# A third place for output panels, doubled weight chunks, and refills at the head of their step in a two-layer encoder trunk

## What is computed

```python
def sq_relu_mlp(h, w_up, w_down):            # d_ff = 4096
    u = relu(h @ w_up)
    return (u * u) @ w_down

# layer 0
x = x + diff_attention(rms_norm(x, attn_norm_g[0]), a_w_qkv, ...)   # 8 heads, ends in  o @ a_w_o
x = x + sq_relu_mlp(rms_norm(x, mlp_norm_g[0]), mlp_w_up[0], mlp_w_down[0])
# shared keys and values
k, v = split(rms_norm(x, kv_norm_g) @ w_kv);  k = rms_norm(k, kv_k_norm_g)
# layer 1
x = x + swa_sink_attention(rms_norm(x, attn_norm_g[1]), b_w_q, ..., b_w_o, k, v)  # 4 groups of 4 query heads
x = x + sq_relu_mlp(rms_norm(x, mlp_norm_g[1]), mlp_w_up[1], mlp_w_down[1])
```

## Time and profile before

| | us |
|---|---|
| median of 3 runs | 2355.66 (2349.65 to 2358.06) |
| the profiled execution | 2355.31 |
| its span, first to last instruction | 2353.6 |
| mean granted clock of PE | 0.975 of full |

### The profile page before, as it was taken

One profiled execution on the slowest core, in us unless ns is written; L12 is line 12 of the kernel. 1 busy time (PEld: TensorE's weight loads), 2 busy tenths in 40 slices (PEclk: granted clock), 3 DMA queues, 4 the chain that ended last, 5 costly groups with the idle time before them and its releaser, 6 DMA issues.

```text
span 2353.6 us, 36507 instructions
## 1 busy us (share of the span) xinstructions
PE 2222.9 (94%) x11916; PEld 1909.4 (81%) x11916; DVE 1593.7 (68%) x3173; ACT 1162.1 (49%) x2483; POOL 842.2 (36%) x1464
## 2 busy tenths in 40 slices
PE   6999999976999999899999989998999999899998
PEld 5999999965878888788777988887878888778777
DVE  5688888763576666776776368875576666776773
ACT  4566666653455455533444256653455555543342
POOL 2333333343642222332334155554542233232331
PEclk9999999977999999999999899997999999999999
DMA  6111000002424444762452110003424444663352
GB/s 197 35 28 28 27 27 21 1 19 93 130 82 148 149 153 161 258 241 84 149 197 90 36 37 10 10 19 99 129 87 155 162 158 162 249 223 104 135 173 82
DMA packets 186756, 255.86 MB, mean 109 GB/s; under 512 B 15072, under 2 KB 135904, under 8 KB 181984
## 3 DMA queue, kind: packets, MB, share of 16 engines
q1 hardware_dynamic: 186592, 253.82, 32.3%
HBM read 174.09 MB, written 79.69 MB: 108 GB/s over the span
## 4 chain that ended last, share of the span: by engine, by line
PE 80%; DVE 10%; issue 5%; ACT 3%; DMA 1%; POOLq 1%; POOL 0%; DVEq 0%; SPq 0%; ACTq 0%
PE score L1855 45%; PE trb L1855 13%; PE proj L1855 13%; PE pv L1855 5%; DVE xop L1350 3%; DVE w_op L1350 1%; PE trb L2205 1%; PE trb L1893 1%; ACT p L960 1%; DVE xT L1591 1%; DVE p L1488 1%; DMA w_quad<-in_mlp_w_down 1%; DVE pb L1802 1%; ACT pb L1315 1%; PE trb L1945 0%
## 5 line engine op out<-in xcount | busy, mean ns | idle before, releaser
L1855 PE MATMUL score<-xop,w_op 128*128 128x512 f32 x3840 | 893.8, 392 | 25.3 <-DVE xop L1350 12.6
L1855 PEld LDWEIGHTS score<-xop,w_op 128*128 128x128 f32 x3840 | 720.8, 189 | 185.3 <-issue 36.1
L799 POOL TENSOR_TENSOR w_quad<-w_quad,w_sum 128x512 f32<-128x512 f32 x64 | 99.5, 1555 | 807.1 <-DVE w_op L1350 807.1
L1855 PE MATMUL trb<-xop,w_op 128*128 128x512 f32 x1536 | 361.9, 390 | 5.4 <-DVE w_op L1350 2.0
L1855 PEld LDWEIGHTS trb<-xop,w_op 128*128 128x128 f32 x1536 | 287.4, 188 | 68.8 <-issue 5.8
L923 ACT ACTIVATE w_op<-w_quad 128x512 fp32r<-128x512 f32 (+1 forms) x336 | 216.3, 645 | 247.0 <-PE score L1855 165.3
L1350 DVE TENSOR_TENSOR w_op<-w_quad,w_op 128x512 fp32r<-128x512 f32 (+1 forms) x336 | 285.0, 852 | 43.8 <-ACT w_op L923 43.8
L1591 DVE TENSOR_TENSOR xT<-score,xT 128x512 f32<-128x512 f32 x160 | 109.8, 686 | 159.0 <-PE score L1855 150.9
L1855 PE MATMUL score<-a_hi,w_op 128*128 128x512 f32 x512 | 162.1, 397 | 3.8 <-DVE w_op L1350 3.8
L960 ACT ACTIVATE p<-p,nm_a,slopes 128x128 f32<-128x128 f32 (+7 forms) x124 | 106.6, 861 | 112.6 <-DVE nm_a L1493 110.4
L1350 DVE TENSOR_TENSOR xop<-xop 128x1024 fp32r<-128x1024 f32 x112 | 143.3, 1290 | 16.3 <-ACT xop L923 16.3
(11 more groups left out here) (266 smaller groups left out, 4567.1 us busy)
## 6 DMA issues: line engine op xcount, KB each, us to landing
xop<-u_dram SPq DMA_DIRECT2D x112, 512.0 KB, 5.8
u_dram<-quad SPq DMA_DIRECT2D x32, 1536.0 KB, 9.7
w_quad<-in_mlp_w_up SPq DMA_DIRECT2D x64, 512.0 KB, 5.3
w_quad<-in_mlp_w_down SPq DMA_DIRECT2D x64, 512.0 KB, 4.9
wa_raw<-in_a_w_qkv SPq DMA_DIRECT2D x96, 128.0 KB, 2.4
quad<-xT_dram SPq DMA_DIRECT2D x32, 256.0 KB, 4.2
xT_dram<-xs SPq DMA_DIRECT2D x32, 256.0 KB, 2.6
u_dram<-quad SPq DMA_DIRECT2D x32, 256.0 KB, 4.0
```

The costliest lines, as they stand in the source:

```text
L799: return pool.tensor_tensor(out, x, y, ALU.subtract)
L1855: return nc.tensor.matmul(out, a, b, start=start, stop=stop, **kw)
```

## The change

In four parts.

**Panels.** The split weights have three places, in slots (2, 3), (0, 1) and (5, 6) of `w_op`, and the results three pairs of banks, the third made of `proj` and `pv`. PE may begin panel i once panel i - 3 has been added. Panel 2 of layer 0 is split at the end of the first attention. The split of a panel moves one panel earlier in ACT's and DVE's order, and its load with it. The last panel is done by halves: first the 24 matmuls of tokens 512 to 1023, then those of the first half, of which 16 read only `a_hi` and the last 8 read `a_lo`. The weights of the MLP's products 3 and 4 (ACT) and 3 (DVE) and the scaling of the last panel's second half move ahead of its first half, and slots 2 and 3 of `xop23` are released at the end of the `a_hi` products.

**Weight chunks.** Chunks 0 to 5 of odd jobs live in `wo_b`, so chunks 0 to 5 of a job are split while the job before runs (in one piece for jobs 1 and 2, two chunks in each of steps 2, 3 and 4 for jobs 3 to 5), and chunks 6 and 7 where all eight stood.

**Refills.** Each half slot from the fourth on stands a step earlier, apart from those that share one, and in its step the refill stands first on ACT, and on DVE behind the additions and ahead of `op_of_weights`.

**Loops.** The `Fori` over groups 1 and 2 is written out.

```diff
@@ refill_at
-    steps = (1, 2, 4, 5, 6, 7, 8, 8, 9, 10, 11, 11, 12, 13)
+    steps = (1, 2, 4, 4, 5, 6, 7, 7, 8, 9, 10, 10, 11, 12)
@@ tiles and banks
-        w_hi = [w_op[:, 2 * i, :, :].rearrange("p a (k n) -> p (a k) n", n=P) for i in range(2)]
-        w_lo = [w_op[:, 2 * i + 1, :, :].rearrange("p a (k n) -> p (a k) n", n=P) for i in range(2)]
+        w_hi = [w_op[:, i, :, :].rearrange("p a (k n) -> p (a k) n", n=P) for i in (2, 0, 5)]
+        w_lo = [w_op[:, i, :, :].rearrange("p a (k n) -> p (a k) n", n=P) for i in (3, 1, 6)]
+        wo_bank = [bank[0], bank[1], [proj[:, :], pv[:, :]]]
+        def halves_of(i):
+            return (1, 0) if i == KC - 1 else (0, 1)
+        def wb_rows(part, k, job):
+            if job % 2 and k < 6:
+                return wo_b[:, k // 2, part, 256 * (k % 2):256 * (k % 2 + 1)]
+            return (wb_hi, wb_lo)[part][:, k, :]
@@ sync, segment
                 load_wo(0)
                 load_wo(1)
+                load_wo(2)
                 if seg == 0:
-                    load_wo(2)
                     load_wo(3)
...
+                if seg:
+                    load_wo(3)
                 for i in range(KC):
-                    if i + 2 < KC and (seg or i >= 2):
-                        load_wo(i + 2)
+                    if 1 <= i < KC - 3:
+                        load_wo(i + 3)
@@ scalar
             square_outputs(NH * 4, 1, NB - 2)
+            split_panel(2)
             evac_o(last_uses, NH - 1)
-            def wb_split(job, gain):
+            def wb_split(job, gain, first=0, end=KC):
                 act.wait_ge(wb_in, job * 16 + 16)
-                if not isinstance(job, int) or job > 0:
-                    act.wait_ge(pb_ready, job * NB)
-                for k in range(KC):
-                    copy(wb_hi[:, k, :], wb_raw[:, k, :], gains[:, gain, k:k + 1]).then_inc(wb_hi_done, 1)
+                if first < 6 and job == 1:
+                    act.wait_ge(prod, OPS)
+                elif first < 6 and job > 1:
+                    act.wait_ge(pb_ready, (job - 1) * NB)
+                for k in range(first, end):
+                    if k == 6 and job > 0:
+                        act.wait_ge(pb_ready, job * NB)
+                    copy(wb_rows(0, k, job), wb_raw[:, k, :], gains[:, gain, k:k + 1]).then_inc(wb_hi_done, 1)
@@ scalar, segment (vector alike)
-                for i in range(KC):
-                    if i + 1 < KC and (seg or i):
-                        panel = KC * seg + i + 1
-                        split_panel(panel, panel // 2, panel % 2)
-                    if i == KC - 1:
-                        for k in range(3):
-                            op_of_weights(k)
-                        for slot in range(2):
-                            for u in (2, 3):
-                                unit_hi(u, slot)
+                if seg:
+                    split_panel(KC * seg + 1)
+                for i in range(KC - 1):
+                    if i + 2 < KC and (seg or i):
+                        split_panel(KC * seg + i + 2)
                     scaled(i)
-                    if i < KC - 1:
-                        squares(i)
+                    squares(i)
...
-                unit_hi(2, 2)
-                op_of_weights(3)
-                unit_hi(3, 2)
-                op_of_weights(4)
-                squares(KC - 1)
+                for k in range(5):
+                    op_of_weights(k)
+                scaled(KC - 1, (1,))
+                for slot in range(3):
+                    for u in (2, 3):
+                        unit_hi(u, slot)
+                scaled(KC - 1, (0,))
...
                 for k in range(OPS + 6):
+                    for s, h in refill_at(k):
+                        refill_hi(s, h)
                     n = (k + 1) // 7 if k else 0
...
                     if k + LEAD + 1 < OPS:
                         op_of_weights(k + LEAD + 1)
-                    for s, h in refill_at(k):
-                        refill_hi(s, h)
@@ scalar, after segment 0, and steps (vector alike)
+                if s == 5:
+                    wb_split(1, 3, 0, 6)
+            wb_split(1, 3, 6)
...
-                        if s == NB - 2 and more:
-                            wb_split(g + 3, 4)
+                        if s in (2, 3, 4, NB - 2) and more:
+                            wb_split(g + 3, 4, *((6, KC) if s == NB - 2 else (2 * s - 4, 2 * s - 2)))
...
-            with act.Fori(1, KVH - 1) as g:
+            for g in range(1, KVH - 1):
@@ vector, MLP step
+                    for s, h in refill_at(k):
+                        refill_lo(s, h)
                     if k < 4:
                         for u in (2, 3):
                             unit_lo(u, 3 + k)
                     if k + LEAD < OPS:
                         op_of_weights(k + LEAD)
...
-                    for s, h in refill_at(k):
-                        refill_lo(s, h)
@@ tensor
+            def last_panel(slot):
+                out, w_h, w_l = wo_bank[slot], w_hi[slot], w_lo[slot]
+                for k in range(KC):
+                    last = three(out[1], (w_h[:, k, :], w_l[:, k, :]), (a_hi[:, k, HALF:S], a_lo[:, k, HALF:S]),
+                                 k == 0, k == KC - 1)
+                last.then_inc(panel_half, 1)
+                for k in range(KC):
+                    mm(out[0], w_h[:, k, :], a_hi[:, k, 0:HALF], k == 0, False)
+                    last = mm(out[0], w_l[:, k, :], a_hi[:, k, 0:HALF], False, False)
+                    if k in (3, KC - 1):
+                        last.then_inc(wo_half, 1)
+                for k in range(KC):
+                    last = mm(out[0], w_h[:, k, :], a_lo[:, k, 0:HALF], False, k == KC - 1)
+                last.then_inc(panel_half, 1)
...
-                    if i >= 2:
-                        pe.wait_ge(xs_ready, 16 * seg + 2 * i - 2)
+                    if i >= 3:
+                        pe.wait_ge(xs_ready, 16 * seg + 2 * i - 4)
```

More of the change, by code:

```diff
@@ L601, in segment @@
                         load_unit(u)
-                    for half in range(2):
-                        sp.wait_ge(xs_ready, 16 * seg + 2 * i + half + 1)
+                    for j, half in enumerate(halves_of(i)):
+                        sp.wait_ge(xs_ready, 16 * seg + 2 * i + j + 1)
                         sp.dma_start(x_dram[:, i, HALF * half:HALF * (half + 1)], xs[:, half, :])\
@@ L1137, in squares @@
                 def squares(i):
-                    for half in range(2):
+                    if i == KC - 1:
+                        act.wait_ge(panel_half, 2 * KC * (seg + 1))
+                    for half in halves_of(i):
                         if i % 2 and i < KC - 1:
@@ L1581, in _, with wb_split @@
             o_factors(NH, 1)
-            def wb_split(job, gain):
-                for k in range(KC):
+            split_panel(2)
+            def wb_split(job, gain, first=0, end=KC):
+                for k in range(first, end):
                     dve.wait_ge(wb_hi_done, job * KC + k + 1)
-                    low(wb_lo[:, k, :], wb_raw[:, k, :], wb_hi[:, k, :], gains[:, gain, k:k + 1])\
+                    low(wb_rows(1, k, job), wb_raw[:, k, :], wb_rows(0, k, job), gains[:, gain, k:k + 1])\
                         .then_inc(wb_lo_done, 1)
@@ L1604, in unit_lo, with add_x @@
                     low(x_part(slot, u, 1), quad[u % 2][:, slot, :], x_part(slot, u, 0)).then_inc(op_split, 1)
-                def add_x(i):
+                def add_x(i, halves=(0, 1)):
                     u = i // 2
-                    for half in range(2):
-                        dve.wait_ge(panel_half, 2 * KC * seg + 2 * i + half + 1)
+                    for half in halves:
+                        dve.wait_ge(panel_half, 2 * KC * seg + 2 * i + halves_of(i).index(half) + 1)
                         dve.wait_ge(quad_in[u % 2], 64 * (2 * seg + u // 2 + 1))
@@ L1613, in add_x @@
                             dve.wait_ge(x_sq, 32 * seg + 2 * i + half - 1)
[L1614 removed]
+                        add(xs[:, half, :], wo_bank[i % 3][half], quad[u % 2][:, TILE[i % 2, half], :]).then_inc(xs_ready, 1)
                 dve.wait_ge(o_split, seg * KC + EARLY[seg])
@@ L1633, in segment @@
                             unit_lo(i // 2 - 1, slot)
-                unit_lo(2, 2)
-                op_of_weights(3)
-                unit_lo(3, 2)
+                for k in range(4):
+                    op_of_weights(k)
+                add_x(KC - 1, (1,))
+                for slot in range(2):
+                    for u in (2, 3):
+                        unit_lo(u, slot)
+                add_x(KC - 1, (0,))
+                for u in (2, 3):
+                    unit_lo(u, 2)
                 def factors():
@@ L2022, in panel_products @@
                 w_h, w_l = w_hi[slot][:, k, :], w_lo[slot][:, k, :]
-                out = bank[slot]
+                out = wo_bank[slot]
```

(2 more changed lines are left out.)

103 lines of the change are left out of this document (54 added, 49 removed).

## The result

The changed kernel takes 2339.3 us against 2356.5 for the one before (six runs of each): ratio 0.9939, 95% interval 0.9924 to 0.9954. It is faster, by 17 us in the medians (14 by the ratio), half or less of the 34 that were forecast, and the time is outside the range of 2308 to 2337. The profiled execution has a time of 2337.1 and a span of 2335.4 us.

What follows compares the result with a forecast made beforehand. The prediction took PE, busy 94% of the span, and its 131 us of idle as the bound. Gains of 5.8 + 3.0 + 13.0 + 12.0 + 0 = 33.8 us off 2355.3 gave 2321.5 us, range 2308 to 2337.

Steps and rivals of the forecast that it cites:

- Term 1: Panels of layer 0: the wait for panel 2's low part and the low clock behind it go; 5.8 us gained.
- Term 3: Weight chunks, second attention: five stalls and their low clock, 14.8 us, go, less 1.8 for added splits; 13.0 us gained.
- Term 5: Six later refill turns: one stall grows from 0.5 to 1.6 us while the next goes; 0 us in all.
- Term 4: First refill turn of each MLP: DVE's 5.7 us of idle go; 6.0 us a layer, 12.0 us gained.
- Term 2: Start of each MLP: the slot 2 stall goes, a second stall grows; 1.5 us a layer, 3.0 us gained.
- Refills that are not the bound: Rival: ACT waits for landings, refill turns and MLP start gain 0; 2336.5 us; chance 0.17.
- A new wait in the second attention: Rival: added splits make DVE the bound of nine steps, costing 7.4 us instead of 1.8; 2327 us; chance 0.10.
- Everything goes: Rival: all named stalls and their low clock vanish, 52.4 us gained; 2302.9 us; chance 0.05.
- Slower: Rival, refill turns: moved refills meet POOL's sums, DVE loses 4.4 us, 32 us lost over 8 turns; 2365 us; chance 0.02.

Runs made afterwards that it cites:

- second profile of the changed kernel: The changed kernel, unaltered, run once more beside the best version: 2347.2 us over ten runs, ratio 0.9953; this profiled execution has a time of 2348.5 us.
- e5: Against E4: half slots 8 and 9 a step earlier in later turns, 6 to 13 earlier in the first turn; 2330.8 us, ratio 0.9890.
- E4: Against the changed kernel: the old refill steps everywhere, refills still first in their step on both engines; 2329.0 us, ratio 0.9892.
- e8: Against the changed kernel: half slots 6 and 7 alone put back from step 7 to step 8; 2325.9 us, one run.
- e10: Against E7: ACT alone takes the new refill steps in each MLP's first turn, DVE keeps the old ones; 2321.4 us, ratio 0.9854.
- e1: Against the changed kernel: without its refill part, so old steps and refills last in their step; 2339.6 us, ratio 0.9933.
- E7: Against E4: DVE's row factors moved from step 4 to step 6, behind an addition PE waits for; 2326.6 us, one run.
- e3: Against the changed kernel: refills last in their step on ACT, still first on DVE, new steps everywhere; 2351.9 us, one run.
- e6: Against E4: three of POOL's four sums in each turn made to wait about 3 steps longer; 2339.0 us, ratio 0.9930.
- e11: Against e10: DVE's weight operations of steps 8 and 9 wait for an addition in step 10, later turns use e5's steps; 2322.5 us, ratio 0.9864.
- e2: Against the changed kernel: refill part kept only in each MLP's first turn, old steps and refills last in later turns; 2332.7 us, ratio 0.9898.

## Why the prediction was wrong

**Term 1 (5.8) was right.** No stall is left before panel 2, and PE reaches the MLP's first `trb` product 5.8 us earlier (4.8 to 6.1 over the thirteen profiles of kernels with the new panels).

**Term 3 (13.0) held in its mechanism and came out smaller: 11.3.** The five stalls on `wb_lo` in jobs 1 to 5 are gone; what is left of `wb_lo` belongs to job 0. The waits for `kTb_lo`, `wTb_lo` and `vb` take back some 3.6 us (4.2, 3.4 and 1.1 against 3.6, 1.5 and none) where 1.8 was allowed. The 11.3 is on the good side by luck: the stretch took 424.0 us before, and 412.2 to 416.6 in the thirteen profiles with the same code there, so the gain is 7.4 to 11.8 by one profile of the kernel before. In the second profile of the changed kernel (416.6) PE is busy for 388.0 us there and in the one shown for 383.1, with the same matmuls, so that difference is low clock; in e5, as long, it is busy for 385.1, so there waits count as well. What the written-out loops brought by themselves, put at 0 in the forecast, no run shows.

**Term 5 failed first: "so one more refill (1.13) stands ahead of that addition".** The count was wrong. I compared the step of the pair and forgot that those before it move too: by the old steps h = 0 to 5 are done ahead of P1, by the new h = 0 to 7, two more. So the stall before S2 grew from 0.48 us to about 2.4, and not to 1.6, and in some turns to 3.6. The one before S3 went, as I said, so without low clock a turn loses only 0.4 us. The term had no low clock at all, though the prediction itself named stalls over 2 us with low clock behind them as a sign of being wrong: that, and the stalls of 3.6, make 5.2 of the 6.8 us lost in the first profile. In the other it is 13.7 (142.0 against 128.3), where 0 was forecast. E4 shows that the steps are the cause, and the profile of e8 that the pair is: put back, the loss is gone.

**Term 4 failed at "it is inside the 5.7, since it is the same chain".** The 5.7 us that DVE waited for ACT fell to 1.5, and the second piece of the turn became 5.0 and 4.3 us shorter. But S4's wait comes earlier on PE than what the chain gains: its growth from 0.8 to 2.06 and 1.71 came on top, in layer 0 with low clock behind it (7.31 for 5.71 us), and in layer 1 a wait of 2.26 with low clock was left before S3. The first turns gained 3.8 and 3.4 us, not 6.0 each. E4 and e10 show that both can be had: old steps on DVE keep S4 at 0.6, ACT's early steps remove the wait before A12, and 5.5 and 6.0 us are won, the 6.0 of the forecast.

**Term 2 was mis-sized: 0.4 for 3.0.** The stall at slot 2 went as said, 1.6 us in each layer. But the wait before S4 grew from 0.52 to 2.02 in layer 0, since DVE's 2 us of row factors stand ahead of that addition, which I had counted as part of a chain of operations slowed by POOL. The low clock came anyway: in layer 0 it moved from behind slot 2 (7.35 us for 24 matmuls before, 5.72 after) to behind S4 (4.29 for 12). In layer 1 the wait went from 2.00 to 1.34 only because PE came later: the clock was granted at 0.75 and 0.83 in the two stretches of 4 us from 1700 to 1708, ahead of it, and from the start at slot 2 to the start of S4 it is 11.35 us, as in e1 (11.38), where PE waited 2.04. In six other profiles it was 2.00 to 2.04 there, with the low clock behind it. E7 shows the cause: with the factors moved behind the addition, no stall is left before S4 in either layer.

**The rivals.** *Refills that are not the bound* named the wait that came (72 us of ACT for landings) and the time nearly (2336.5), but by luck: e3 takes 57 us of those waits away and the stalls of PE stay. *A new wait in the second attention* came in part, 3.6 us by the waits where that rival had 7.4. *Everything goes* did not come: the stalls before S2 and S4 stand. *Slower* fell with its mechanism: DVE loses 1.27 + 1.09 = 2.4 us to POOL in the turn shown, and 3.3 where the pair takes 4.59, against 2.1 before and the 4.4 that it asked for. E4, where the slowing is 2.2 us and the later turns are shorter than before the change, shows that PE pays for the place ahead of P1 and not for the slowing by itself. The Trainium skill (SBUF — State Buffer, Who interferes with whom) has DVE and GpSimd exclude each other for such operations; e6 agrees in that both grow where they overlap (0.68 to 1.78 on DVE, 1.3 to 2.1 to 2.3 on POOL) and in that the slowing follows POOL's place.

## What to carry to other kernels

When a schedule moves many items by a step, count for each addition on the path how many stand ahead of it before and after, over all of them, and not only the item that is next to it. Give each engine its own steps. The engine that only copies can take the earlier ones, if its waits for input hold up nothing that others need; the engine that also frees banks takes the later ones (e10, in the first turns). Where a stall grows past 2 us, price the low clock that may follow it too. And a stretch in which one engine is full does not get shorter by reordering inside it: in e5, e6 and e11 the stall only got another name or place.

## What the runs showed of the hardware that was not expected

The same stall does not always bring the low clock. Before S4 of the first pair in layer 0, PE waited 2.02 us in the changed kernel's first profile and 2.04 in its second, with the same code, and its next 12 matmuls took 4.29 us and 2.96. With the same order of work there, e5 waited 2.01 and took 4.19, and e1, e4 and e8 waited 2.00 to 2.04 and took 2.96 to 3.00. In layer 1, though, a stall of 2.00 to 2.02 or 2.04 at the same place was followed by 4.57 or 4.58 us in each of the six profiles that had it (e1, e2, e4, e5, e6 and the second of the changed kernel), while the kernel before waited 2.00 and took 3.00. So a stall of about 2 us costs between 2 and 3.6 us, and a price for the clock behind it is an average.

For the stalls before S2 in the later turns (both profiles of the changed kernel and e3): of eleven of 2.36 to 2.43 us, three had low clock behind them; of seven of 3.59 to 3.66 us, all had.

A short operation of DVE loses as much beside POOL as a long one: 128x512 elements go from 0.68 to 1.78 us, and the pair of 128x1024 from 2.35 to 3.5, or to 4.5 where both meet it. That is about 1.1 us at most for each that meets a sum of POOL; one refill in e6 lost 0.5.
